# Attention stage: where the mixing and the scores stand among the products of a unit, and in which order the probabilities' parts are made

## What is computed

```python
q, k, v = split(h @ w_in, 3)                   # 16 heads of width 64
for each head, each chunk of 64 queries:        # keys: own chunk and the 8 before
    s = q @ k.T * 64**-0.5 + bias               # masked outside the band
    p = softmax(s)
    o = p @ v
x = x + o @ w_out
```

## Time and profile before

| | |
|---|---|
| median of 3 runs | 1864.22 us (1864.22 to 1864.34) |
| profiled execution, its own time | 1864.35 us |
| its span, first to last instruction | 1862.6 us |
| TensorE (PE) busy | 1840.3 us, 99% of the span |
| VectorE (DVE), GpSimd (POOL), ScalarE (ACT) busy | 61%, 51%, 45% |
| granted clock of TensorE, mean | 0.999 |
| 16 DMA engines, mean | 100 GB/s |

### The profile page before, as it was taken

One profiled execution on the slowest core, in us unless ns is written; L12 is line 12 of the kernel. 1 busy time (PEld: TensorE's weight loads), 2 busy tenths in 40 slices (PEclk: granted clock), 3 DMA queues, 4 the chain that ended last, 5 costly groups with the idle time before them and its releaser, 6 DMA issues.

```text
span 1862.6 us, 24027 instructions
## 1 busy us (share of the span) xinstructions
PE 1840.3 (99%) x9444; PEld 1569.4 (84%) x9444; DVE 1133.1 (61%) x1816; ACT 843.1 (45%) x1318; POOL 944.5 (51%) x407
## 2 busy tenths in 40 slices
PE   9999999999999999999999999999999999999998
PEld 7778889898888888888889898998888887888886
DVE  6987775775776333433565445457777766454546
ACT  5345343342354233332454545355666645443544
POOL 5673466475443434333448566574222327674755
PEclk9999999999999999999999999999999999999999
DMA  5222414424232222222243232403333332423221
GB/s 187 91 91 68 153 51 155 151 76 151 68 113 68 91 91 91 68 91 90 83 165 114 68 136 68 136 28 99 101 101 110 103 101 80 136 78 126 91 91 57
DMA packets 142764, 187.10 MB, mean 100 GB/s; under 512 B 4000, under 2 KB 102576, under 8 KB 142528
## 3 DMA queue, kind: packets, MB, share of 16 engines
q1 hardware_dynamic: 135392, 172.76, 28.1%
q10 hardware_dynamic: 7264, 12.86, 2.4%
HBM read 179.28 MB, written 6.33 MB: 100 GB/s over the span
## 4 chain that ended last, share of the span: by engine, by line
PE 80%; DVE 9%; ACT 3%; issue 1%; POOL 1%; DMA 0%; ACTq 0%; DVEq 0%
PE ps L688 26%; PE ps L690 26%; PE ps L689 26%; DVE ps L2066 1%; POOL w_lo L667 1%; ACT w_hi L1198 1%; DVE work L2408 1%; DVE diagonals L1734 1%; DVE xl L1760 0%; DVE probs_t_lo L2427 0%; PE ps L1077 0%; DVE work L2421 0%; PE ps L1011 0%; DVE work L2004 0%; DVE q_hi L2398 0%
## 5 line engine op out<-in xcount | busy, mean ns | idle before, releaser
L667 POOL TENSOR_TENSOR w_lo<-raw,w_hi 128x1024 fp32r<-128x1024 f32 x244 | 591.1, 2431 | 754.9 <-ACT w_hi L1198 754.9
L688 PE MATMUL ps<-xh,w_hi 128*128 128x512 f32 x1408 | 554.0, 393 | 4.9 <-DVE xl L1760 2.7
L690 PE MATMUL ps<-xh,w_lo 128*128 128x512 f32 x1408 | 548.2, 389 | 0.0
L689 PE MATMUL ps<-xl,w_hi 128*128 128x512 f32 x1408 | 548.2, 389 | 0.0
L1198 ACT ACTIVATE w_hi<-raw 128x1024 fp32r<-128x1024 f32 x262 | 273.2, 1057 | 427.9 <-PE ps L690 397.6
L688 PEld LDWEIGHTS ps<-xh,w_hi 128*128 128x128 f32 x1408 | 264.4, 188 | 64.4 <-issue 8.0
L689 PEld LDWEIGHTS ps<-xl,w_hi 128*128 128x128 f32 x1408 | 264.4, 188 | 55.3 <-issue 1.9
L690 PEld LDWEIGHTS ps<-xh,w_lo 128*128 128x128 f32 x1408 | 264.3, 188 | 55.3
L688 PE MATMUL ps<-hid_hi,w_hi 128*128 128x256 f32 (+1 forms) x688 | 228.3, 332 | 1.8 <-DVE hid_lo L2010 0.7
L690 PE MATMUL ps<-hid_hi,w_lo 128*128 128x256 f32 (+1 forms) x688 | 227.1, 330 | 0.0
L689 PE MATMUL ps<-hid_lo,w_hi 128*128 128x256 f32 (+1 forms) x688 | 227.0, 330 | 0.0
(11 more groups left out here) (272 smaller groups left out, 3095.8 us busy)
## 6 DMA issues: line engine op xcount, KB each, us to landing
raw<-in_mlp_w_dram SPq DMA_DIRECT2D x40, 1024.0 KB, 5.4
raw<-in_ret_w_in_dram SPq DMA_DIRECT2D x24, 1024.0 KB, 5.2
work<-in_mlp_w_dram SPq DMA_DIRECT2D x16, 1024.0 KB, 5.7
raw<-in_att_w_in_dram SPq DMA_DIRECT2D x12, 1024.0 KB, 5.5
raw<-in_w_gate_dram SPq DMA_DIRECT2D x11, 1024.0 KB, 5.3
raw<-in_w_up_dram SPq DMA_DIRECT2D x11, 1024.0 KB, 5.5
raw<-in_w_in_dram SPq DMA_DIRECT2D x9, 1024.0 KB, 5.1
raw<-in_ret_w_out_dram SPq DMA_DIRECT2D x8, 1024.0 KB, 5.1
```

The costliest lines, as they stand in the source:

```text
L667: nc.gpsimd.tensor_tensor(half_of(wl[:, b % 2, :], b, half), half_of(source, b, half), half_of(wh[:, b % 2, :], b, half).bitcast(F32), ALU ...
L688: nc.tensor.matmul(o, a[0], b[0], start=first, stop=False, skip_group_check=True)
L689: nc.tensor.matmul(o, a[0], b[1], start=False, stop=False, skip_group_check=True)
L690: return nc.tensor.matmul(o, a[1], b[0], start=False, stop=last, skip_group_check=True)
```

## The change

TensorE: the mixing of the head before and the scores of the head after move from behind the unit into its middle, after 12 of its 24 matmuls (`between`, which `unit8` already had and `unit4` gets). For s = 3 the scores of the next group's first head stay behind the unit. For s = 0 both stand ahead of the unit of v. In the last group the scores of head 14 stay ahead of the unit.

ScalarE and VectorE: the order inside a head follows. For s = 1 and s = 2, `probs_hi` and `probs_lo` of head h now stand ahead of the exponentials and the normalising of head h + 1, and for s = 1 the parts of the unit's q come last.

```diff
@@ tensor @@
+                    if between and (m, k) == (1, 1):
+                        between()
...
                         if s == 0:
                             qk_unit(3)
+                            mix(h - 1)
+                            scores(h + 1)
                             unit_v(X)
-                            scores(h + 1)
-                            mix(h - 1)
                             turn(h)
                             continue
...
                         if last_group and s == 1:
                             scores(h + 1)
+
+                        def inside():
+                            if s == 1:
+                                pe.wait_ge(unit_taken, v_units)
+                            mix(h - 1)
+                            if s == 2 or s == 1 and not last_group:
+                                scores(h + 1)
+
+                        if last_group:
                             pe.wait_ge(mix_ready, 8)
-                            unit4_narrow(s - 1)
+                            unit4_narrow(s - 1, inside)
                         else:
...
+                            qk_unit(s - 1, inside)
+                            if s == 3:
                                 scores(h + 1)
...
                         turn(h)
@@ scalar @@
                             mixed_copy(h - 1)
+                            exps(h + 1)
                             v_unit(0)
-                            exps(h + 1)
                             probs_hi()
...
+                        if last_group:
+                            if s == 1:
+                                exps(h + 1)
+                            mixed_copy(h - 1)
+                            after_unit()
+                            probs_hi()
+                            if s == 2:
+                                exps(h + 1)
+                        else:
+                            mixed_copy(h - 1)
+                            if s > 1:
+                                qk_unit(s - 1)
+                            probs_hi()
                             exps(h + 1)
...
+                            if s == 1:
+                                qk_unit(0)
                         mixed_hi(h - 1)
@@ vector @@
                             mixed_add(h - 1)
+                            normalise(h + 1)
                             value_lo()
-                            normalise(h + 1)
                             probs_lo()
...
+                        elif s == 3:
+                            mixed_add(h - 1)
+                            qk_taken(2)
+                            maxima(h + 1)
+                            qk_lo(2)
+                            probs_lo()
+                            normalise(h + 1)
                         else:
+                            maxima(h + 1)
+                            mixed_add(h - 1)
                             qk_taken(s - 1)
...
                             if s == 2:
-                                qk_lo(s - 1)
...
+                                qk_lo(1)
+                            probs_lo()
                             normalise(h + 1)
-                        probs_lo()
+                            if s == 1:
+                                qk_lo(0)
                         mixed_lo(h - 1)
```

More of the change, by code:

```diff
@@ L717, in unit8, with unit4 @@
                 c.unit.n += 1
-            def unit4(rhs, k0, ready=None, fresh=1, bank0=None, last=None):
+            def unit4(rhs, k0, ready=None, fresh=1, bank0=None, last=None, between=None):
                 slot, half = c.unit.n // 2 % 2, c.unit.n % 2
@@ L1038, in qk_unit, with unit4_narrow @@
                         unit8(X, slot=(slot0 + n % 2) % 2, half=n // 2, ahead=(1, 2, 0, 1)[n], between=between)
-                    def unit4_narrow(n):
-                        unit4(H, 0, fresh=0, bank0=0)
+                    def unit4_narrow(n, between=None):
+                        unit4(H, 0, fresh=0, bank0=0, between=between)
                     def scores(h):
@@ L1120, in _ @@
                             scores(h + 1)
+                        def inside():
[5 more added lines that the diff above has]
+                        if last_group:
                             pe.wait_ge(mix_ready, 8)
-                            unit4_narrow(s - 1)
+                            unit4_narrow(s - 1, inside)
                         else:
[L1124 to L1128, removed]
+                            qk_unit(s - 1, inside)
+                            if s == 3:
                                 scores(h + 1)
-                        if s == 1:
-                            pe.wait_ge(unit_taken, v_units)
-                        mix(h - 1)
                         turn(h)
@@ L1665, in _ @@
                             v_unit(1)
-                        if last_group and s == 1:
-                            exps(h + 1)
[L1668 to L1678, removed]
+                        if last_group:
[11 more added lines that the diff above has]
+                            probs_hi()
+                            exps(h + 1)
+                            if s == 1:
+                                qk_unit(0)
                         mixed_hi(h - 1)
@@ L2482, in _ @@
                             value_lo()
[L2483 to L2490, removed]
+                        if last_group:
+                            if s < 3:
                                 maxima(h + 1)
                             mixed_add(h - 1)
-                            if h + 1 < ATT_HEADS:
+                            if s == 1:
                                 normalise(h + 1)
-                        else:
+                            out_narrow(s - 1)
+                            probs_lo()
+                            if s == 2:
+                                normalise(h + 1)
[5 more added lines that the diff above has]
+                            probs_lo()
+                            normalise(h + 1)
+                        else:
+                            maxima(h + 1)
+                            mixed_add(h - 1)
                             qk_taken(s - 1)
-                            maxima(h + 1)
                             if s == 2:
-                                qk_lo(s - 1)
-                            mixed_add(h - 1)
-                            if s != 2:
-                                qk_lo(s - 1)
+                                qk_lo(1)
+                            probs_lo()
                             normalise(h + 1)
-                        probs_lo()
+                            if s == 1:
+                                qk_lo(0)
                         mixed_lo(h - 1)
```

## The result

The changed kernel takes 1891.63 us (median of 4; 1890.44 to 1891.87) against 1864.28 before (median of 4): 27.3 us more, a ratio of 1.0144 with a 95% interval of 1.0131 to 1.0158. The forecast was 1883 with a range of 1873 to 1890. The direction was right, and the time lies 1.6 us above the range.

The account below looks back on a forecast made before the run. TensorE, busy 99% of the span, bounds the kernel, and its old waits, 7.1 us, are all that can be won. New waits of 26.2 less 7.1 give +19.1 on 1864.35: 1883 us, range 1873 to 1890.

Parts of the forecast that it names:

- M(0): Mixing of head 0 on TensorE, now half a unit behind its turning, waits for the low parts: +4.2 us.
- M(1), M(5), M(9): Mixing of heads 1, 5, 9: low parts ready at 1.9 us, mixing comes at 2.8, so no wait: 0.
- T(2), T(6), T(10): Turnings of heads 2, 6, 10 wait for maxima behind a mixed low part GpSimd blocks: 2.1 us each, +6.2.
- M(2), M(6), M(10): Mixing of heads 2, 6, 10 waits for late low parts, behind unit 1's parts and DMA issues: 3.5 each, +10.5.
- T(3), T(7), T(11): Turnings of heads 3, 7, 11, with scores directly ahead, wait for the maxima: 0.5 us each, +1.6.
- M(3), M(7), M(11): Mixing of heads 3, 7, 11, a whole unit behind: low parts ready 0.2 us ahead; 0, upper end 1.5.
- last group: Output units wait for both banks to be added, with only a turning between; also low-part waits: together +3.7 us.
- waits of before, gone: TensorE's old waits over the four windows, 7.1 us, all the change can win; gone where maxima start in time.
- every term is a wait: Whole sum: no instruction is added or removed, so every term of the change is a wait.
- The clock falls: Rival: after idling 3.5 to 4.2 us, the half unit behind runs at 1.2 GHz, four times: 1894; chance 0.08.
- If the issues cost nothing, 1.3 less each: Lower end for the mixing of heads 2, 6, 10: free DMA issues would make it 3.8 in all.
- GpSimd loses the port race: Rival: maxima in time, turnings of head 2 and its like don't wait, 6.2 less: 1877; chance 0.18.

Follow-up runs that it names:

- e3: The changed kernel with the two DMAs copying unit 1's high part issued behind the high parts of the probabilities of heads 2, 6 and 10: 1889.54 us.
- e4: The changed kernel with ScalarE's half of the weights at heads 1, 5 and 9 moved behind the mixed high part and the next mixed copy: 1884.95 us.
- e6: The changed kernel with the heads of s = 2 and s = 3 put back to the order of before on all engines: 1897.98 us.
- the best version: The kernel before with probabilities' parts ahead of exponentials and normalising, head 0's parts first, some mixed low parts behind later maxima; TensorE order unchanged: 1858.82 us.
- e8: Mixed version: the change's TensorE order for s = 0 and 1, the old one elsewhere, head 0's parts first, some ScalarE and VectorE work reordered: 1878.20 us.
- e5: The changed kernel with 12 small matmuls of ones ahead of the wait for the low parts at heads 0, 2, 6 and 10: 1883.42 us.
- e1: The changed kernel with 24 small matmuls of ones ahead of the wait for the low parts at heads 0, 2, 6 and 10: 1889.46 us.

## Why the prediction was wrong

By its steps, with what the changed kernel's timeline shows from start to start:

| term | forecast | measured |
|---|---|---|
| M(0) | 4.2 | 4.35 |
| M(1), M(5), M(9) | 0 | 0 |
| T(2), T(6), T(10) | 6.2 | 5.0 (1.64 to 1.68 each) |
| M(2), M(6), M(10) | 10.5 | 10.6 (3.5 each) |
| T(3), T(7), T(11) | 1.6 | 1.7 |
| M(3), M(7), M(11) | 0 | 0 |
| last group | 3.7 | 3.5 |
| waits of before, gone | -7.1 | -7.1 (taken as forecast) |
| no wait: scores behind a mixing take 1.34 us, not 1.28, and the like | 0 | about 1 (the rest of the 19.0) |
| slow clock | 0 | 8.7 |

- **What failed is the step "every term is a wait"**: the sum put the slow clock at nothing. It stood apart as the rival "The clock falls", with a chance of 0.08, and was left out of the range. The rival put the cost at 11 us and the time at 1894; it was 8.7, and the time 1891.6. The sign named for being wrong is what came: matmuls of 128x512 0.43 us apart. What the rival needed stood in the prediction itself: four waits of 3.5 to 4.2 us, when no wait of rows 3 is over 0.5. That no row showed such a fall was no evidence against it, since no row had such a wait. Here the rule of the Trainium skill that it cited (TensorE: Matmul & The Clock Gate, What's actually happening) is what the trace then showed: the granted clock is 0.50 behind each long wait and comes back to 1.00 some 3.5 to 6.5 us after work resumed. It is 0.50 from the first matmul on at M(2) and M(10); at M(6) it is 1.00 at first and 0.50 from 0.6 us on.
- **The chains of waits held**, four of them within 0.2 us a place, though both M terms are the longest chains of the text. T(2) waited 1.64 and not 2.1: GpSimd was through 8.4 us after T(1), not 8.6, the maxima began at 8.8, not 9.2, and TensorE came to the turning at 8.15, not 8.0. That all waits together came to 19.0 where 19.1 was forecast is in part luck: the 1.2 us too much at T(2) and its like are made up by the 1 us that the sum had nowhere.
- **"If the issues cost nothing, 1.3 less each"** was wrong: e3 shows 0.46. The issue gap was in the chain, but another stood beside it, VectorE's low parts of the unit. A lower end has to be worked out on both engines.
- **"GpSimd loses the port race"** was rightly refused: GpSimd asked at 1334.17, while the mixed high part was done only at 1334.61, and e4 shows what the port was worth, 4.8 us.
- **"M(3) ... value 0"** was right for this kernel, but with little room: the low parts were done at 1360.66 and M(3) began at 1361.06, and that only because T(3) was late; e6 turned it into 3.8 us.
- **The sum of the old waits**, 7.1 us as all that can be won, held as a bound: the best version wins 5.8.

## What to carry to other kernels

Work that moves from behind a long piece to its middle, or from behind one to ahead of it, loses that piece as cover: list the chain that feeds it on every engine and set its length against what is left, for each head of a group, not for the first that comes to mind, and again once the others are mended. Look in that chain for VectorE's subtractions beside a GpSimd instruction: one of 0.69 us took 2.8 here. Where a sum holds a wait several times longer than any the trace has, price the slower clock behind it too; filling the wait with matmuls that compute nothing is a quick test of how much of a loss is clock. And if the small waits are all there is to win, start with what makes their releaser late: here a few lines on ScalarE and VectorE won what the move on TensorE was to bring.

## What the runs showed of the hardware

- The granted clock of TensorE fell to 0.50 behind idle times of 4.1, 3.8 and 3.4 us every time, though not always at once: at M(6) of e4 (idle for 3.44) the whole mixing still ran at full speed, 1.35 us, and the unit behind it did not. It also fell after waits of 2.93 to 2.98 us in e3 and e8, in e8 at two of three places only in the middle of the scores behind M (matmuls of 128x512 0.43 us apart from 1353.9 on, after M(3) had run at full speed). It stayed at 1.00 after the waits of 2.08 us in e6. How long the slow stretch lasts differs from place to place in one kernel, 1.5 to 2.9 us of cost in the changed one, and the runs with such stretches scatter more: 1883.65 to 1886.42 in e4, against 1883.15 to 1884.15 in e5, which has none.
- A matmul of fp32 ones, 128x128, takes 0.22 us from start to start (24 in 5.27 us in e1), twice what a transpose of the same size takes (0.10 us in a turning); the trace has two records for each.
- ScalarE issues DMAs beside running activations where they need not wait for its own result: in e3 the two issues lie beside the high parts and cost ScalarE nothing; ahead of them, with a wait for its own copy, they cost it 1.27 us.
